# Running sums over later key blocks in a stick-breaking attention, and four weight slabs split on GpSimd

## The reference, cut to what matters

```python
def block(i):                       # Q_BLOCK = 128 queries
    z = einsum('bthd,bshd->bhts', qb, k) * scale
    causal = key_pos[None, :] < qpos[:, None]
    log_beta = jax.nn.log_sigmoid(z)
    log_1mb = jnp.where(causal, jax.nn.log_sigmoid(-z), 0.0)
    later = lax.cumsum(log_1mb, axis=3, reverse=True) - log_1mb
    attn = jnp.where(causal, jnp.exp(log_beta + later), 0.0)
    return einsum('bhts,bshd->bthd', attn, v)
```

## Time and profile before

| | us |
|---|---|
| median of 3 runs | 740.01 (739.89 to 740.15) |
| the profiled execution | 739.92 |
| its span | 738.2 |
| TensorE busy | 729.7 (99%) |
| VectorE busy | 521.7 (71%) |
| ScalarE busy | 335.5 (45%) |
| GpSimd busy | 226.2 (31%) |

### The profile page before, as it was taken

The page is one execution under the profiler, slowest core; times in us unless marked ns, Lnnn a source line. Parts: engine busy times, 40 slices in busy tenths (PEclk is TensorE's granted clock), DMA queues, the critical chain, the costliest instruction groups (busy, mean ns, idle before and its releaser), DMA issues.

```text
span 738.2 us, 9798 instructions
## 1 busy us (share of the span) xinstructions
PE 729.7 (99%) x3506; PEld 581.6 (79%) x3506; DVE 521.7 (71%) x736; ACT 335.5 (45%) x480; POOL 226.2 (31%) x193
## 2 busy tenths in 40 slices
PE   8999999999999999999999999999999999999998
PEld 4778878787777666688888988888888888888886
DVE  5354796899996756556655569695978869595972
ACT  5234744365665877633224353524435252534320
POOL 2013424200002565003301073634527090715610
PEclk9999999999999999999999999999999999999999
DMA  9307423310111212133091134242240605131102
GB/s 328 137 15 181 162 68 104 115 44 15 58 57 58 58 58 58 57 104 114 11 316 55 58 115 157 71 133 96 93 134 13 213 2 170 57 114 57 57 15 101
DMA packets 43894, 70.64 MB, mean 96 GB/s; under 512 B 2641, under 2 KB 27217, under 8 KB 43858
## 3 DMA queue, kind: packets, MB, share of 16 engines
q1 hardware_dynamic: 43858, 70.17, 29.4%
HBM read 65.71 MB, written 2.10 MB: 92 GB/s over the span
## 4 chain that ended last, share of the span: by engine, by line
PE 93%; ACT 2%; DVE 2%; POOL 1%; issue 1%; DMA 0%; SPq 0%; DVEq 0%; ACTq 0%
PE ps L1741 7%; PE ps L1742 7%; PE ps L1743 7%; PE ps L408 7%; PE ps L415 6%; PE ps L417 6%; PE ps L416 6%; PE ps L410 6%; PE ps L1769 6%; PE ps L409 6%; PE ps L1770 6%; PE ps L1771 6%; PE ps L1579 2%; PE ps L1623 2%; PE ps L1655 1%; PE ps L1665 1%
## 5 line engine op out<-in xcount | busy, mean ns | idle before, releaser
L1741 PE MATMUL ps<-b_hi,cut_hi 128*128 128x512 f32 (+1 forms) x280 | 104.0, 371 | 0.0
L1742 PE MATMUL ps<-b_lo,cut_hi 128*128 128x512 f32 (+1 forms) x280 | 103.8, 371 | 0.0
L1743 PE MATMUL ps<-b_hi,cut_lo 128*128 128x512 f32 (+1 forms) x280 | 103.8, 371 | 0.0
L415 PE MATMUL ps<-cut_hi,a_hi 128*128 128x512 f32 x224 | 89.9, 402 | 1.0 <-DVE a_lo L1006 1.0
L417 PE MATMUL ps<-cut_hi,a_lo 128*128 128x512 f32 x224 | 87.7, 391 | 0.0
L416 PE MATMUL ps<-cut_lo,a_hi 128*128 128x512 f32 x224 | 87.4, 390 | 0.0
L399 DVE TENSOR_TENSOR cut_lo<-raw,cut_hi 128x2048 fp32r<-128x2048 f32 (+2 forms) x36 | 59.1, 1641 | 32.2 <-ACT cut_hi L391 32.2
L876 ACT ACTIVATE qo_sb<-ps 128x512 f32<-128x512 f32 x32 | 19.1, 598 | 135.4 <-PE ps L1743 90.8
L615 POOL TENSOR_TENSOR a_lo<-qo_sb,a_hi 128x512 fp32r<-128x512 f32 x49 | 78.2, 1623 | 5.6 <-ACT a_hi L886 5.6
L603 POOL TENSOR_SCALAR qo_sb<-qo_sb 128x128 f32<-128x128 f32 (+3 forms) x28 | 33.3, 1188 | 118.9 <-DVE snmax L1181 117.9
L391 ACT ACTIVATE cut_hi<-raw 128x2048 fp32r<-128x2048 f32 (+2 forms) x33 | 49.3, 1494 | 32.8 <-PE ps L410 22.7
(11 more groups left out here) (192 smaller groups left out, 1650.7 us busy)
## 6 DMA issues: line engine op xcount, KB each, us to landing
raw<-in_w_ff_dram SPq DMA_DIRECT2D x32, 1024.0 KB, 5.5
raw<-in_w_in_dram SPq DMA_DIRECT2D x16, 1024.0 KB, 5.4
gates<-in_x_dram SPq DMA_DIRECT2D x8, 512.0 KB, 5.9
raw<-in_w_out_dram SPq DMA_DIRECT2D x4, 1024.0 KB, 5.1
raw<-in_w_in_dram SPq DMA_DIRECT2D x4, 512.0 KB, 6.3
raw<-in_w_branch_sb_dram SPq DMA_DIRECT2D x2, 1024.0 KB, 5.1
raw<-in_w_branch_sa_dram SPq DMA_DIRECT2D x4, 512.0 KB, 6.1
out_dram<-gates SPq DMA_DIRECT2D x8, 256.0 KB, 2.0
```

The costliest lines, as they stand in the source:

```text
L415: nc.tensor.matmul(dst, l_hi, w_hi, start=start, stop=False)
L1741: T.matmul(dst, w_hi[:, w], b_hi[:, k, a:b], start=(k == 0), stop=False)
L1742: T.matmul(dst, w_hi[:, w], b_lo[:, k, a:b], start=False, stop=False)
L1743: mm = T.matmul(dst, w_lo[:, w], b_hi[:, k, a:b], start=False, stop=(k == KD - 1))
```

## The change

In the stick-breaking stage VectorE makes running sums in lg after each softplus: columns of block 3 are added to block 2, and then those of block 2 to block 1, wherever both have the same query block. With R the running sum, TensorE needs for key block 0 the triangle on block 0 and ones on R of block 1; for key block i from 1 on, the triangle on R of block i, which counts the later blocks by the triangle too, and `below` (ones minus triangle) on R of block i + 1, which completes them. That is seven block products a head, in 10 fp32r and 2 f32 matmuls. The matrix below is made once at the start, on VectorE, in f32 (over the mask's place) and fp32r.

Of the two top-k steps between the heads one moves behind the second head. In the last stage it isn't made up for, so one more step falls into the softmax loop. The lower parts of slabs 11 to 14 move from VectorE to GpSimd, all four ahead of its fifth bias; VectorE waits for their semaphore ahead of its next cut, at n = 5.

```diff
-        const_r = sb("const_r", [P, 2, P], F32R)
-        tri_r, ones_r = const_r[:, 0, :], const_r[:, 1, :]
+        below_f = mask_f
+        const_r = sb("const_r", [P, 3, P], F32R)
+        tri_r, ones_r, below_r = (const_r[:, j, :] for j in range(3))
...
             for n in range(32):
+                if n == 4:
+                    for i in range(SL_GATE + 1, SL_GATE + 5):
+                        pool.wait_ge(hi_done, i + 1)
+                        pool.wait_ge(lo_done, i)
+                        pool.tensor_tensor(cut_lo[:, i % CUT, :], raw[:, i % RAW, :], cut_hi[:, i % CUT, :].bitcast(F32),
+                                           ALU.subtract).then_inc(lo_done, 1)
...
-            V.tensor_copy(mask_b, mask_f).then_inc(const_cut, 1)
+            link(V.tensor_copy(mask_b, mask_f))
+            link(V.tensor_tensor(below_f, ones_f, tri_f, ALU.subtract))
+            V.tensor_copy(below_r, below_f).then_inc(const_cut, 1)
...
                 link(V.scalar_tensor_tensor(out=buf, in0=zset(h), scalar=0.0, in1=buf, op0=ALU.max, op1=ALU.add))
+                for j in (2, 1):
+                    here, after = buf[:, ZCOL[j] + P:ZCOL[j] + (4 - j) * P], buf[:, ZCOL[j + 1]:ZCOL[j + 1] + (3 - j) * P]
+                    link(V.tensor_tensor(here, here, after, ALU.add))
...
                 softplus(2 * c + 1)
-                topk(2)
+                topk(1)
                 softplus_cut(2 * c + 1)
-                dve_cut(SL_GATE + 1 + c)
...
-                topk((8, 6, 5, 0)[c])
+                topk((9, 7, 6, 0)[c])
...
                 if n % 8 in (5, 6) and n < 32:
+                    if n == 5:
+                        dve.wait_ge(lo_done, SL_GATE + 5)
                     dve_cut(SL_GATE + 5 + n // 8, n % 8 - 5, 2)
...
                 for i in range(4):
-                    for j in range(i, 4):
-                        a = ZCOL[j]
+                    for j in range(i, min(i + 2, 4)):
+                        a, last = ZCOL[j], j == min(i + 1, 3)
                         if j == 3:
-                            mm = T.matmul(zt(h, i, j), tri_f if i == j else ones_f, lg[:, h % 2, a:a + P],
+                            mm = T.matmul(zt(h, i, j), tri_f if i == j else below_f, lg[:, h % 2, a:a + P],
                                           start=False, stop=True, skip_group_check=True)
                             continue
-                        for part in (sp_hi, sp_lo):
-                            mm = T.matmul(zt(h, i, j), tri_r if i == j else ones_r, part[:, a:a + (4 - j) * P],
-                                          start=False, stop=False, skip_group_check=True)
+                        with_r = tri_r if i == j else ones_r if i == 0 else below_r
+                        T.matmul(zt(h, i, j), with_r, sp_hi[:, a:a + (4 - j) * P],
+                                 start=False, stop=False, skip_group_check=True)
+                        T.matmul(zt(h, i, j), with_r, sp_lo[:, a:a + (4 - j) * P],
+                                 start=False, stop=last, skip_group_check=True)
```

More of the change, by code:

```diff
@@ L992, in _ @@
             V.memset(cold_b[:, :], 0.0)
-            V.tensor_copy(const_r[:, :, :], const_f[:, 0:2, :])
+            V.tensor_copy(const_r[:, 0:2, :], const_f[:, 0:2, :])
             V.tensor_copy(ident_b, ident[:, :])
-            V.tensor_copy(mask_b, mask_f).then_inc(const_cut, 1)
+            link(V.tensor_copy(mask_b, mask_f))
+            link(V.tensor_tensor(below_f, ones_f, tri_f, ALU.subtract))
+            V.tensor_copy(below_r, below_f).then_inc(const_cut, 1)
             def norm_scale(m, dst, src, g):
```

## The result

The changed kernel takes 741.39 us (median of 18 runs, 741.16 to 742.81) against 739.99 (18 runs, 739.82 to 740.15). The ratio is 1.0023, with a 95% interval from 1.0016 to 1.0031: slower by 1.4 us, small but clear of noise. The prediction said 740.0 and no change; the time lies in its range, on the side that had the least chance.

What follows compares the result with a forecast made beforehand. TensorE's row of matmuls was taken as the bound. Heads save 0.68 us each, but a 3.9 us wait and VectorE's chain leave 0.13 us late: 739.92 plus 0.13, 740.0 us, range 735.8 to 742.0.

Steps and rivals of the forecast that it cites:

- the side that had the least chance: Whole kernel: measurably slower than before, by at least 1.5 us; chance 0.16, against 0.34 faster and 0.50 same.
- The removed products: TensorE, eight attention heads: three block products go, 2.68 to 2.00 us a head, 5.4 us in all if nothing waits.
- The hold: First stage: GpSimd's 4.55 us subtraction keeps VectorE's first sum waiting to about 158.95; TensorE starts head 1 at 163.38.
- The later stages: Third and fourth attention stages: each gains 0.90 us of the 1.36 its heads save, VectorE's chain between heads being longer.
- the 0.5 to 1 us named as a sign: Later stages: TensorE waits this long for sp_lo before each odd head, with no stretched sum.
- the sum: Whole kernel, full hold: 0.13 us late after the fourth stage, the rest at nothing, so 740.0 us.
- the hole: First stage: TensorE stands still 3.9 us before head 1, from 159.50, waiting for sp_lo.
- the slower rival: TensorE's clock falls in the first-stage wait; some 4 us of matmuls at half speed, 2 to 4 us lost, 742 to 744; chance 0.12.
- the main case: Whole kernel as forecast: full GpSimd hold, no clock loss, 740.0 us, own range 739.2 to 741.0; chance 0.52.

Runs made afterwards that it cites:

- the last experiment: Changed kernel with GpSimd's first lower part waiting for head 1's sp_lo, and no top-k step between a stage's heads: 734.14 us, ratio 0.9923.
- the hole filled: Changed kernel with 16 matmuls of zeros into an unused bank ahead of head 1's products, where TensorE stood still: 740.25 us, ratio 1.0006.
- both orders tried: Changed kernel, four lower parts back on VectorE, top-k steps behind second heads 8, 6, 5, 0: 739.90 us; with 8, 7, 6, 1: 739.88 us.

## Why the prediction was right or wrong

**The removed products, 0.68 us a head: right.** 1.99 us a head in place of 2.68, and the last experiment turns all eight into time.

**The hold: right, in its size too.** GpSimd's instruction was put at 4.55 us from 154.5 and took 4.62 from 154.41; the first sum was to wait until 158.95 and was let go at 158.9; TensorE was to start head 1 at 163.38 and did at 163.32. Here I had extended a hold of 1.3 us, the longest that a row showed, to 4.55. The Trainium skill (SBUF — State Buffer, "Who interferes with whom") says that the first to issue has the shared ports for the whole instruction, and the run agrees: 4.28 us for a sum of 0.29. The same section of the Trainium skill counts copies among the instructions that can take the shared ports; the rows of before left that open, and the copy of 2.14 us beside GpSimd agrees with it.

**The later stages, 0.90 us each: right within 0.1.** With the clock out of the way the odd heads stood at 185.00, 206.24 and 227.49, against 185.00 and 206.2 in the working for the first two; from odd head to odd head that is 21.24 and 21.25 us in place of 22.11 and 22.08 before. The waits before the odd heads were shorter than the 0.5 to 1 us named as a sign: 0.35 and 0.34 in the third and fourth stage of the change, none in its second.

**The step that failed: the sum gives head 1 its full-speed 2.00 us behind the hole, and nothing for TensorE's clock.** It took 3.66. The change is 1.4 us above the kernel before. With the hole filled it is 0.4 above, near the 0.1 of the sum; the other 1.0 us came because TensorE fell to its lower level behind the hole. I had this as the slower rival, at 0.12, with 2 to 4 us. All 18 runs show it by a mean clock of 0.998 or 0.995 and by their times, none of which is under 741.16 (with the hole filled, none is above 740.47), so it belonged in the main case. I had argued only that a gap of 1.03 us did nothing, which says little on one of 3.9. Its size was also off: the slow stretch takes 1.6 us more on TensorE, and in the usual runs only 0.9 reach the end, as the second stage had slack before head 3. In the other seven runs the mean clock is lower and the time 0.7 to 1.5 us above the usual runs' 741.3. No profile of such a run was taken, so where and how long the clock was low there is not shown; the mean also counts the time behind the last matmul, where several profiles have 0.50.

**What I saw too late.** The working treated VectorE's order as given. It had found that VectorE's chain between the heads is longer than TensorE's, but that one more top-k step moved behind the heads would give 2.2 us was seen only in the experiments. And the GpSimd part, costed at nothing beside the hold, is what makes the sums affordable: with the lower parts on VectorE the whole gain was lost in both orders tried.

**Open.** What decides in a given run whether the clock falls after a gap of 1.9 or 2.4 us was not tried, and neither was what sets the change's seven slower runs apart. What makes up the 0.3 us between the sum and the kernel with its hole filled is only in part traced: at the end of the eight heads it is 0.26 us late (229.78 against 229.52) where the sum had 0.13.

## What to carry to other kernels

Before moving work to an idle GpSimd, list what VectorE does in the time of that one instruction: here an instruction with two inputs in SBUF, or a plain copy in SBUF, that came after it waited for its end, and the longer the GpSimd instruction, the longer the wait. Place it by a semaphore behind the VectorE work that others wait for; here that one wait was worth 4.9 us. And where TensorE is the bound, a hole of 2 us or more can cost more than its length, through the clock; and look first at which VectorE work between two urgent steps could stand behind the second.

## What the runs showed of the hardware that was not expected

- TensorE's clock fell in mid-kernel after gaps shorter than I had in mind. After a wait of 3.79 us it fell in 18 of 18 runs, by mean clock and time; after one of 2.40 us in 7 of 11 and after one of 1.94 us in 4 of 11, if the upper group of times is taken for it, as the one profile of each shows. After waits of 1.28 us and less from 20 us on (the longest of them near 20.3 us in the kernel in quarters) no profile shows a slow matmul.
- The fall need not start with the first matmul behind the gap: after 1.94 us the clock held for another 0.9 us of matmuls and fell then. With GpSimd's cut in quarters it had fallen before head 1 started at 162.12: by windows of one microsecond it was 0.96 from 161 on and 0.50 from 162 on.
- Matmuls of zeros that nobody uses kept it: 1.0 us gained by 16 of them.
- An fp32 copy from SBUF to SBUF waited for GpSimd as a two-input instruction does (2.14 us in place of 0.83). The softplus instruction, with one input in PSUM, did not: in the second stage of the changed kernel it started while GpSimd's instruction ran, 0.43 us before that one's end, and took its usual 1.49 us. Nor did the top-k steps beside it (0.56 and 0.54 us, as elsewhere).

```profile
171.12 4.63 POOL L599 TENSOR_TENSOR cut_lo<-raw,cut_hi 128x2048 fp32r<-128x2048 f32 x1 [12.09 <-ACT cut_hi L392]
...
173.18 0.56 DVE L1046 MAX8 best<-topm 128x8 f32<-128x384 f32 x1
...
173.86 0.54 DVE L1047 MATCH_REPLACE8 topm<-best,topm 128x384 f32<-128x384 f32 x1
175.32 1.49 DVE L1166 SCALAR_TENSOR_TENSOR lg<-ps,lg 128x1280 f32<-128x1280 f32 x1 [0.92 <-ACT lg L776]
```
